# Sums of the weights' blocks on VectorE, the fourth block split earlier, and the sample's convolution spread out, in a decoder-layer kernel

## The reference

```
h = rms_norm(x, g_mix_pre);  z = h @ w_in
y_a = pool_mixer(z[.., :256]);  y_b = conformer_conv(z[.., 256:768]);  y_c = chunk_spatial_gating(..);  y_d = short_gated_conv(..)
x = x + rms_norm(concat(y_a, y_b, y_c, y_d) @ w_out, g_mix_post)
f = rms_norm(x, g_ffn_pre)
f = square(relu(f @ w_up)) @ w_down          # w_up 1024 x 4096, w_down 4096 x 1024
x = x + rms_norm(f, g_ffn_post)
# conformer_conv: g = p * sigmoid(gate); c = causal depthwise conv of 31 taps + bias;
#                 layer norm over each head of 64 channels; silu
```

## Time and profile before

| | us |
|---|---|
| median of 3 runs (2219.36 to 2226.23) | 2220.45 |
| profiled execution | 2222.52 |
| its span | 2220.8 |
| TensorE busy | 2076.3 (93%) |
| VectorE busy | 1415.5 (64%) |
| ScalarE busy | 897.7 (40%) |
| GpSimd busy | 310.7 (14%) |

### The profile page before, as it was taken

How to read it: one execution, slowest core, us unless ns; L and a number is a source line. 1 busy time by engine, 2 the same in 40 slices (tenths; PEclk the granted TensorE clock), 3 DMA queues, 4 the chain that set the end, 5 groups by cost and what they waited for, 6 DMA issues and landing times.

```text
span 2220.8 us, 33082 instructions
## 1 busy us (share of the span) xinstructions
PE 2076.3 (93%) x13769; PEld 1881.7 (85%) x13769; DVE 1415.5 (64%) x1946; ACT 897.7 (40%) x1478; POOL 310.7 (14%) x262
## 2 busy tenths in 40 slices
PE   6999999996799999998999999899999999999998
PEld 5877777785688888988888899798888989999998
DVE  3687786866667685468577646677585465334344
ACT  4424242234535443455435344535443453323142
POOL 3011110110132140004032200133130000000000
PEclk9999999997999999999999999999999999999999
DMA  7754556553132324443332345332324334222221
GB/s 251 278 209 170 211 179 216 192 182 105 50 115 76 114 77 135 137 155 105 114 115 67 105 152 171 114 115 76 114 83 145 98 117 152 77 96 76 96 77 60
DMA packets 185418, 287.44 MB, mean 129 GB/s; under 512 B 6543, under 2 KB 162868, under 8 KB 177060
## 3 DMA queue, kind: packets, MB, share of 16 engines
q1 hardware_dynamic: 161444, 169.99, 23.8%
q0 software_dynamic: 22784, 114.28, 14.6%
q10 hardware_dynamic: 1040, 1.05, 0.1%
HBM read 245.01 MB, written 40.57 MB: 129 GB/s over the span
## 4 chain that ended last, share of the span: by engine, by line
PE 44%; DVE 15%; DMA 6%; ACT 6%; issue 5%; POOL 0%; DVEq 0%; ACTq 0%; POOLq 0%
PE mm L2259 14%; PE mm L2261 14%; PE mm L2260 14%; DVE w_lo L1401 5%; DVE w_lo L1396 3%; ACT w_hi L867 2%; DMA raw<-in_w_ffn_up 2%; DMA raw<-in_w_ffn_down 2%; DVE s_lo L1816 1%; ACT w_hi L881 1%; DMA mixc<-mixT_scratch 1%; PE mm L2268 1%; DVE f_sb L1883 1%; PE mm L2267 1%; DVE a_lo L1816 0%
## 5 line engine op out<-in xcount | busy, mean ns | idle before, releaser
L2259 PE MATMUL mm<-act_hi,w_hi 128*128 128x512 f32 (+2 forms) x1728 | 637.4, 369 | 28.9 <-DVE w_lo L1396 22.1
L2261 PE MATMUL mm<-act_hi,w_lo 128*128 128x512 f32 (+2 forms) x1728 | 634.6, 367 | 0.0
L2260 PE MATMUL mm<-act_lo,w_hi 128*128 128x512 f32 (+2 forms) x1728 | 629.2, 364 | 0.0
L1396 DVE TENSOR_TENSOR w_lo<-raw,w_hi 128x2048 fp32r<-128x2048 f32 x116 | 265.8, 2292 | 356.4 <-ACT w_hi L867 356.1
L2259 PEld LDWEIGHTS mm<-act_hi,w_hi 128*128 128x128 f32 x1728 | 329.8, 191 | 83.5 <-DVE w_lo L1396 23.9
L2260 PEld LDWEIGHTS mm<-act_lo,w_hi 128*128 128x128 f32 x1728 | 330.2, 191 | 57.7 <-issue 2.4
L2261 PEld LDWEIGHTS mm<-act_hi,w_lo 128*128 128x128 f32 x1728 | 329.4, 191 | 51.8
L867 ACT ACTIVATE w_hi<-raw 128x2048 fp32r<-128x2048 f32 x116 | 221.8, 1912 | 306.9 <-PE mm L2261 130.0
L2259 PE MATMUL mm<-w_hi,u_hi 128*128 128x256 f32 x896 | 248.8, 278 | 0.5 <-DVE u_lo L1808 0.2
L2260 PE MATMUL mm<-w_lo,u_hi 128*128 128x256 f32 x896 | 247.5, 276 | 0.0
L2261 PE MATMUL mm<-w_hi,u_lo 128*128 128x256 f32 x896 | 247.4, 276 | 0.0
(11 more groups left out here) (306 smaller groups left out, 3520.8 us busy)
## 6 DMA issues: line engine op xcount, KB each, us to landing
raw<-in_w_ffn_up SPq DMA_DIRECT2D x64, 1024.0 KB, 5.3
raw<-in_w_ffn_down SPq DMA_DIRECT2D x72, 512.0 KB, 4.2
raw<-in_w_ffn_down SPq DMA_DIRECT2D x28, 1024.0 KB, 5.1
w_hi<-whi_scratch POOLq DMA_DIRECT2D x24, 1024.0 KB, 5.2
w_lo<-wlo_scratch POOLq DMA_DIRECT2D x24, 1024.0 KB, 7.7
raw<-in_w_out SPq DMA_DIRECT2D x16, 1024.0 KB, 5.1
whi_scratch<-w_hi POOLq DMA_DIRECT2D x8, 1024.0 KB, 8.9
wlo_scratch<-w_lo POOLq DMA_DIRECT2D x8, 1024.0 KB, 11.1
```

The costliest lines, as they stand in the source:

```text
L1396: DVE.tensor_tensor(w_lo[:, s, :, :], raw[:, r // 2, :, :], w_hi[:, s, :, :].bitcast(fp32), ALU.subtract)\
L2259: PE.matmul(out, whi, xhi, start=(k == 0), stop=False)
L2260: PE.matmul(out, whi, xlo, start=False, stop=False)
L2261: return PE.matmul(out, wlo, xhi, start=False, stop=(k == K - 1))
```

## The change

The four sums of a weight panel are issued by VectorE, at new places in its order; GpSimd keeps its DMAs. Block b22 is the fifth part and the third sum the sixth, where they were sixth and fifth; the products, the places of the seven sums over the hidden width and SP's waits follow. In stages of q=0 ScalarE copies the banks (`w_copy`), where VectorE did. In the first block the sample's taps are spread over all up panels, the mean lies behind up panel 3, and the rest of the chain inside the first stage.

```diff
@@ shared: places of the sums over d_ff, order of the blocks
+        m6, m7 = (mixc[:, i, :, :].rearrange("p k t -> p (k t)").rearrange("p (h c) -> p h c", h=2) for i in range(2))
+        m4 = f2_sb[:, NCH, :].rearrange("p (h c) -> p h c", h=2)
+        m2, m3, m1, m5 = (f2_sb[:, t:t + 2, c:c + D // 2] for t, c in ((0, 0), (0, D // 2), (2, 0), (2, D // 2)))
+        w_sum = [m1, m2, m5, m7, m3, m6, m4]
-            return quarter(raw, (b11, b21, b11, b12, b11, b22, b21)[i])
+            return quarter(raw, (b11, b21, b11, b12, b22, b11, b21)[i])
@@ SP
+                            sp.wait_ge(w_sums, 4 * w_no[j] - 1)
+                            sp.wait_ge(lo_ready, split_no[j - 1] + 4)
+                            sp.dma_start(quarter(raw, b21), block_source(j, 1, 0)).then_inc(raw_full[b21], 16)
                             sp.wait_ge(w_sums, 4 * w_no[j])
-                            sp.wait_ge(lo_ready, split_no[j - 1] + 4)
+                            sp.wait_ge(lo_ready, split_no[j - 1] + 5)
                             sp.dma_start(quarter(raw, b12), block_source(j, 0, 1)).then_inc(raw_full[b12], 16)
-                            sp.wait_ge(lo_ready, split_no[j - 1] + 5)
-                            sp.dma_start(quarter(raw, b21), block_source(j, 1, 0)).then_inc(raw_full[b21], 16)
...
                     elif order[j - 1][0] == "W":
-                        sp.wait_ge(lo_ready, split_no[j - 1] + 5)
+                        sp.wait_ge(w_sums, 4 * w_no[j - 1] + 3)
+                        sp.wait_ge(lo_ready, split_no[j - 1] + 4)
@@ GpSimd: weight_sums, weight_sum_2, weight_sum_4 and their calls go; conv_s is stored with the others
-                    for m, src in ((3, short_s), (0, pool_ds), (2, us_sb)):
+                    for m, src in ((3, short_s), (0, pool_ds), (2, us_sb), (1, conv_s)):
@@ ScalarE
-                if i == 5:
+                if i == 4:
                     act.wait_ge(raw_full[b22], 16 * raw_no[j][3])
-                if i in (2, 3, 4, 6):
-                    act.wait_ge(w_sums, 4 * w_no[j] + {2: 1, 3: 2, 4: 3, 6: 4}[i])
+                if i in (2, 3, 5, 6):
+                    act.wait_ge(w_sums, 4 * w_no[j] + {2: 1, 3: 2, 5: 3, 6: 4}[i])
...
+            def w_copy(j, i):
+                _, b, q, p = order[j]
+                bank = bank_of[j, i][0]
+                if q == 0:
+                    wait_bank(act, j, i)
+                    if b > 0:
+                        act.wait_ge(y_out, 16 * NCH * b)
+                    else:
+                        act.wait_ge(sx_tr, 1)
+                        act.wait_ge(out_small, 16 * OUT_SMALL)
+                        if i == NS7 - 1:
+                            act.wait_ge(smp_st, 64)
+                    SC.activation(w_sum[i][:, :, p * PC:(p + 1) * PC], mm[bank][:, :].rearrange("p (h c) -> p h c", h=2),
+                                  ACT.Copy).then_inc(bank_free[bank], 1)
...
             def w_panel(j):
+                first = order[j][1:3] == (0, 0)
                 if order[j][3] == 0:
                     for i in range(4, NS7):
                         part_hi(j, i)
+                        w_copy(j, i - 4)
+                        if first and i == 4:
+                            sample_conv_square()
                     for i in range(3):
                         part_hi(j + 1, i)
+                        w_copy(j, i + 3)
+                        if first and i == 0:
+                            sample_conv_root()
+                            sample_swish()
+                    w_copy(j, 6)
                 else:
                     for i in range(3, NS7):
                         part_hi(j, i)
+                        w_copy(j, i - 3)
+                    w_copy(j, 4)
                     split_hi(j + 1)
+                    w_copy(j, 5)
+                    w_copy(j, 6)
                     split_hi(j + 2)
@@ VectorE
+            def weight_sums(j):
+                b11, _, b12, b22 = (quarter(raw, r) for r in raw_at[j])
+                dve.wait_ge(raw_full[raw_at[j][2]], 16 * raw_no[j][2])
+                dve.wait_ge(lo_ready, split_no[j])
+                DVE.tensor_tensor(b11, b12, b11, ALU.subtract).then_inc(w_sums, 1)
+                dve.wait_ge(raw_full[raw_at[j][3]], 16 * raw_no[j][3])
+                dve.wait_ge(w_sums, 4 * w_no[j] + 1)
+                DVE.tensor_tensor(b12, b22, b12, ALU.subtract).then_inc(w_sums, 1)
+            def weight_sum_2(j):
+                b11, _, _, b22 = (quarter(raw, r) for r in raw_at[j])
+                dve.wait_ge(lo_ready, split_no[j] + 2)
+                DVE.tensor_tensor(b11, b22, b11, ALU.subtract).then_inc(w_sums, 1)
+            def weight_sum_4(j):
+                b11, b21, _, _ = (quarter(raw, r) for r in raw_at[j])
+                dve.wait_ge(w_sums, 4 * w_no[j] + 3)
+                DVE.tensor_tensor(b21, b21, b11, ALU.subtract).then_inc(w_sums, 1)
...
             def w_panel(j):
+                first = order[j][1:3] == (0, 0)
                 if order[j][3] == 0:
                     part_lo(j, 2)
-                    if order[j][1:3] != (0, 0):
-                        sum_4(j - 1)
+                    sum_4(j - 1)
+                    w_add(j, 0)
                     part_lo(j, 3)
-                    w_add(j, 0)
                     sums_3(j - 1)
+                    if first:
+                        sample_centre()
                     part_lo(j, 4)
+                    weight_sum_2(j)
                     w_add(j, 1)
                     w_add(j, 2)
                     part_lo(j, 5)
+                    weight_sum_4(j)
                     w_add(j, 3)
                     part_lo(j, 6)
+                    if first:
+                        sample_conv_out()
                     part_lo(j + 1, 0)
                     w_add(j, 4)
                     part_lo(j + 1, 1)
+                    weight_sums(j + 1)
                     w_add(j, 5)
                     part_lo(j + 1, 2)
                     w_add(j, 6)
                 else:
+                    weight_sum_2(j)
                     part_lo(j, 3)
                     w_add(j, 0)
                     part_lo(j, 4)
+                    weight_sum_4(j)
                     w_add(j, 1)
...
@@ VectorE, u_panel ahead of a stage
                     if p < NP - 2:
                         split_lo(j + 2)
+                    elif (b, q) == (0, 0):
+                        sample_taps(range(8, 15) if p == NP - 2 else range(23, TAPS))
                     sums_2(j)
...
                     if p == NP - 2:
+                        if (b, q) == (0, 0):
+                            sample_taps(range(15, 23))
                         part_lo(j + 2, 0)
                         part_lo(j + 2, 1)
+                        weight_sums(j + 2)
@@ VectorE, main loop, b == q == 0: behind up panel p=0 taps 0 to 2 (were 0 to 5), behind p=1 taps 3 to 7 (were 6 to 30)
@@ TensorE
-                   (s_hi[:, 2, :, :], s_lo[:, 2, :, :], 4), (s_hi[:, 1, :, :], s_lo[:, 1, :, :], 5),
-                   (s_hi[:, 3, :, :], s_lo[:, 3, :, :], 6), (a22_hi, a22_lo, 7)]
+                   (s_hi[:, 2, :, :], s_lo[:, 2, :, :], 4), (s_hi[:, 3, :, :], s_lo[:, 3, :, :], 6),
+                   (s_hi[:, 1, :, :], s_lo[:, 1, :, :], 6), (a22_hi, a22_lo, 7)]
...
+                    if (b, q, p, i) == (0, 0, 0, 3):
+                        sample_var()
...
-                    if p == 2:
+                    if p == 3:
                         sample_mean()
-                    if p == 3:
-                        sample_var()
```

More of the change, by code:

```diff
@@ L756, in results @@
                         rows_in("x2", b, i + 2)
[L758 to L781, removed]
-                pool.wait_ge(w_sums, n + 3)
-                pool.wait_ge(lo_ready, split_no[j] + 1)
-                GP.tensor_tensor(b21, b21, b11, ALU.subtract).then_inc(w_sums, 1)
             def sample_out(m, src):
@@ L846, in _ @@
                     store(NB - 1, 1, yb_done, conv[:, (NB - 1) % 2, :, :])
-                    for m, src in ((3, short_s), (0, pool_ds), (2, us_sb)):
+                    for m, src in ((3, short_s), (0, pool_ds), (2, us_sb), (1, conv_s)):
                         sample_out(m, src)
-                for q in range(Q - 1 if b < NB - 1 else 0):
-                    for p in range(NP // 2):
-                        weight_sums(index("W", b, q, p))
-                        if (b, q, p) == (0, 0, 0):
-                            sample_out(1, conv_s)
-                        weight_sum_2(index("W", b, q, p))
-                        weight_sum_4(index("W", b, q, p))
         @block.scalar
@@ L1857, in sums_3 @@
                 block_lo(square[:, 1, 2 * P:4 * P], a22_hi[:, p, :], a22_lo[:, p, :])
-            extra = [f2_sb[:, NCH, :]] + [mixc[:, i, :, :].rearrange("p k t -> p (k t)") for i in range(2)]
-            m1, m6, m7 = (x.rearrange("p (h c) -> p h c", h=2) for x in extra)
```

(34 more changed lines are left out.)

5 lines of the change are left out of this document (removed).

## The result

The changed kernel took 2158.4 us (median of 4 runs, 2157.98 to 2162.1) beside 2222.27 us for the kernel before: a ratio of 0.9715, 95% interval 0.9695 to 0.9735. A second set of runs gave 2158.01 beside 2225.01: 0.9704, 0.9691 to 0.9717. Forecast were 2151 and a range of 2140 to 2182: the sign and the mechanism held, and the gain is 64 us instead of 69. The runs of the kernel before have a median of 2222.27 here, 1.8 us above the 2220.45 from which the forecast was taken. The profiled execution took 2157.98 (span 2156.3), against 2222.52 (2220.8).

What follows compares the result with a forecast made beforehand. TensorE, busy 93% of the span, was taken as the bound, losing time to pauses and half clock. Gains of 46 (six stages q>0), 8 (b=1, 2, q=0) and 15 us (first stage) sum to 69: 2151 us, range 2140 to 2182.

Steps and rivals of the forecast that it cites:

- The pause ahead of a stage of q>0: TensorE's wait for `a_lo` at a stage's first product: 0.25 us instead of 2.19, once GpSimd's sums no longer stretch VectorE.
- The pause behind it: TensorE's wait for the up weights' `w_lo` after a stage: 0 to 0.1 us instead of 2.80, through an earlier load.
- The load of VectorE: VectorE's work in a stage of q>0, with sums, splits and additions: 34.7 of 38.1 us, so it fits.
- slack: Tightest margin between a `w_lo` part being ready and its product's start inside a stage: 0.64 us, at the seventh part.
- The price of a sum: A 128x1024 weight sum on VectorE: 1.22 us with 1.14 between starts; bounds 1.21 and 3.26.
- Rivals B: VectorE's chain is tighter than walked, with sums of 1.7 us: 2168 us; chance 0.27 together with rival A.
- C: Each sum holds VectorE for 2.2 us, as if nothing overlapped: 13 us gained, 2208 us; chance 0.05.
- D: Slower: sums keep GpSimd's price of 2.82 us on VectorE because of the layout of `raw`: 2258 us; chance 0.04.
- The clock: TensorE's granted clock: 1.00 in up panels of 44.15 us; falling as before in stages of b=1, 2, q=0.
- rival A: Pauses shrink but TensorE still falls to 1.2 GHz at the seams: 18 us given back, 2169; chance 0.27 with B.
- The mis-sized term: Ahead of the first stage, the sample's mean on VectorE keeps TensorE waiting 6.0 us; that stretch gains 15 us overall.
- The 0.7 us that I gave to the root and the swish: First stage: the sample's root and swish idle VectorE about 5 us, so the second panel's first part comes 0.7 us late.

Runs made afterwards that it cites:

- the sums on GpSimd: The changed kernel with the four sums of the weights' blocks issued by GpSimd again, all else as changed: 2200.21 us, ratio 0.9895 to the kernel before.
- the doubled splits: The changed kernel with the two splits ahead of the sums in the last up panels done twice in stages of q>0: 2172.46 us, ratio 0.9785.
- Old order: The changed kernel with the old order of block parts and old waits of SP's loads, sums staying on VectorE: 2194.21 us, ratio 0.9864.
- one more operation: The changed kernel with the split of the first panel's seventh part done twice in the six stages of q>0: 2163.64 us, ratio 0.9734.

## Why the prediction came out so

- **The pause ahead of a stage of q>0**: walked 0.25, measured 0.26 to 0.28. The cause named, GpSimd's sum beside `s_sum` and `a_lo`, is shown by the sums on GpSimd, and VectorE's queue as what the stage waits for by the doubled splits.
- **The pause behind it**: walked 0 to 0.1, measured 0 five times and 0.17 once. Old order: 3.2, as the walk of the chain gives.
- **The load of VectorE**: walked 34.7 of 38.1 us, measured 34.2; slack walked 0.64, and with one more operation the pause is 0.58.
- **The price of a sum**: taken 1.22, measured 1.22 on average with 1.14 to 1.32 between starts. Rivals B, C and D fell with it: `s_sum` starts 1.14 us behind the start of the second sum, not 2.2. Beside its flush the section that I set against the change (the Trainium skill, VectorE: DVE Perf Modes, "The DRAIN you can't avoid") says that a next operation that is not held starts earlier, which I had left out. But even the second sum, which waits by a semaphore for the first, starts 1.32 us behind it, and there the measurement decides against the flush.
- **The clock**: the up panels run at 1.00 (rival A fell) and the stages of b=1, 2 at 0.94, as forecast. What I had taken for A, that the stages at 699.55 and 790.15 took the same and so "two limits lie close together", was a misreading: the one was long by short pauses and a slower pace, the other by half clock in most of its first product.
- **The mis-sized term**: "`sample_mean` still holds TensorE for 6.0 us". It holds it for 8.3. I let VectorE begin the last two up panels on time, but it came late from the sample's work in p=0 and p=1. Three rows of the changed kernel's VectorE and TensorE, then one of VectorE in the run with the taps in the output projection:

```profile
583.20 0.42 DVE L1859 TENSOR_TENSOR s_sum<-square 128x256 f32<-128x256 f32 x1
...
596.00 2.68 DVE L2177 SCALAR_TENSOR_TENSOR conv_s<-gs_ext,cst,conv_s 128x32 f32<-128x32 f32 x16
...
598.74 1.06 PE L2286 MATMUL tr<-conv_s,headmean 128*128 128x32 f32 x4 [8.26 <-DVE conv_s L2177]
...
581.20 0.43 DVE L1859 TENSOR_TENSOR s_sum<-square 128x256 f32<-128x256 f32 x1 [1.73 <-ACT square L1130]
```

  This `s_sum` starts 3.92 us behind the end of up panel p=2 (579.28); without the taps it starts 1.50 us behind it (579.70), after 1.73 us of idle time. So VectorE is 2.4 us late. The 2.3 us of taps that stand ahead of it there would alone make 0.6 of that; the rest it brings along from p=0 and p=1. The last taps end as much later: 8.4 us behind the end of the up panels (590.33), where I had walked 5.9. The 0.7 us that I gave to the root and the swish inside the stage did not show. Net, the first stage gave 13.2 instead of 15.
- **A reading**: the 0.60 us per addition in the load of VectorE is the distance between starts, which a timeline shows; the row that I gave for it has 0.678. The sum is right.
- The other 2.3 us of the miss in the gain lie in stretches without an edit. Two profiles of this same kernel have spans of 2156.3 and 2160.3 us, so they need no cause of their own; I have none.

What stays open is why the matmuls keep a pace of 0.1178 us behind some pauses inside a stage, and why the clock fell behind three of six like pauses in the kernel before.

## What to carry to other kernels

Walk the queue of the engine that feeds the bound one, in the order of the code, with starts and not only durations; for the change it gave pauses to a tenth of a microsecond, and missed where it was started from an engine that was already late. For the experiments it also missed the waits inside a stage that come of a late load (old order) and the ones behind it that come of a stretched split (sums on GpSimd). Before two engines are given work on the same memory, see in a timeline whether the small operations of one end just behind the large ones of the other. Parts of a change can fail to add, as here, so try each alone and all together.

## What the runs showed of the hardware

- A pause inside a stage can cost more than itself at a granted clock of 1.00: behind it, matmuls of 128x256 start every 0.1178 us instead of 0.1133, to the stage's end. It followed 4 of 6 pauses of 0.6 us in one run, and the kernel before has it behind a pause of 0.47 us.
- The clock's fall does not follow from a pause's length. With stages of an unbroken 38.1 us around it, a pause of 2.8 us left it at 1.00 six times of six in the profiled run. Ahead of the six stages of q>0 of the kernel before, pauses of 2.2 us left it at 1.00 three times and three times not (0.96). With the old order, behind 3.08 us it read 0.94 and behind 3.11 us 1.00.
- A VectorE operation of 0.42 us took 2.6 us beside a GpSimd sum, and the GpSimd sum 3.26 instead of 2.36 when VectorE came first.
